# One mLSTM layer on one core: the per-head squares go from ScalarE to GpSimd, and a few steps at stage starts change places

## The reference

```
u = rmsnorm(x, mix_norm_g)
q, k, v, o_pre, gates = split(u @ w_in)          # 8 heads, 64 wide for q and k, 128 for v
per head, causal and stabilised:
    h = num / max(|den|, exp(-m))                # num 128 wide per head, den one number
h = merge_heads(_rms(h)) * norm_g                # _rms: divide by sqrt(mean(h^2) + 1e-6), per head
x = x + (h * sigmoid(o_pre)) @ w_out
x = x + (silu(n @ w_gate) * (n @ w_up)) @ w_down # n = rmsnorm(x, ffn_norm_g), 2816 wide inside
```

## Time and profile before

| what | value |
|---|---|
| median of the runs | 2179.42 us |
| the profiled execution | 2179.42 us, of which the span is 2177.8 us |
| PE busy | 2126.1 us, 98% of the span |
| PEld, DVE, ACT, POOL busy | 1766.0, 1431.5, 939.2, 252.5 us |
| chain that ended last | PE 89%, DVE 6%, ACT 2%, DMA 1% |
| granted TensorE clock, mean | 0.994 |

### The profile page before, as it was taken

One profiled execution on the slowest core, in us unless ns is written; L12 is line 12 of the kernel. 1 busy time (PEld: TensorE's weight loads), 2 busy tenths in 40 slices (PEclk: granted clock), 3 DMA queues, 4 the chain that ended last, 5 costly groups with the idle time before them and its releaser, 6 DMA issues.

```text
span 2177.8 us, 29479 instructions
## 1 busy us (share of the span) xinstructions
PE 2126.1 (98%) x10440; PEld 1766.0 (81%) x10440; DVE 1431.5 (66%) x2274; ACT 939.2 (43%) x1686; POOL 252.5 (12%) x357
## 2 busy tenths in 40 slices
PE   5999999999999999999999999899999999999999
PEld 4888878888888888788878888788888888888887
DVE  8775466686656565579687644767865756556764
ACT  4443664453333333345444346543533333333443
POOL 4111100020101010100122111001110101001000
PEclk8999999999999999999999999999999999999999
DMA  4333364213233324863524334532223332357443
GB/s 146 102 116 106 98 238 145 88 49 121 97 116 101 116 92 142 295 229 113 155 68 140 96 102 155 213 136 78 68 97 116 101 109 95 100 197 245 149 132 109
DMA packets 200289, 281.56 MB, mean 129 GB/s; under 512 B 12913, under 2 KB 131697, under 8 KB 200177
## 3 DMA queue, kind: packets, MB, share of 16 engines
q1 hardware_dynamic: 171696, 183.07, 26.6%
q0 software_dynamic: 28480, 97.02, 12.7%
HBM read 197.73 MB, written 82.31 MB: 129 GB/s over the span
## 4 chain that ended last, share of the span: by engine, by line
PE 89%; DVE 6%; ACT 2%; DMA 1%; issue 1%; SPq 0%; POOL 0%; DVEq 0%; POOLq 0%; ACTq 0%
PE ps L2179 13%; PE ps L2181 13%; PE ps L2182 13%; PE ps L1920 7%; PE ps L1924 7%; PE ps L1922 7%; PE ps L2227 6%; PE ps L2231 6%; PE ps L2229 6%; PE ps L1833 2%; PE ps L1835 2%; PE ps L1834 2%; PE ps L1840 1%; DMA g_in<-ops_hbm 1%; PE ps L2098 1%
## 5 line engine op out<-in xcount | busy, mean ns | idle before, releaser
L1671 DVE TENSOR_TENSOR ring<-raw_f,ring 128x512 fp32r<-128x512 f32 x308 | 211.4, 687 | 187.6 <-ACT ring L1107 186.5
L1107 ACT CAST ring<-raw_f 128x512 fp32r<-128x512 f32 x308 | 191.1, 622 | 208.0 <-PE ps L2182 194.0
L2179 PE MATMUL ps<-u_lo,ring 128*128 128x512 f32 x704 | 275.6, 391 | 2.2 <-DVE u_lo L1268 2.2
L2182 PE MATMUL ps<-u_hi,ring 128*128 128x512 f32 x704 | 274.1, 389 | 0.0
L2181 PE MATMUL ps<-u_hi,ring 128*128 128x512 f32 x704 | 273.9, 389 | 0.0
L2227 PE MATMUL ps<-ring,ring 128*128 128x512 f32 x616 | 240.9, 391 | 7.1 <-DVE ring L1750 7.1
L2229 PE MATMUL ps<-ring,ring 128*128 128x512 f32 x616 | 239.8, 389 | 0.0
L2231 PE MATMUL ps<-ring,ring 128*128 128x512 f32 x616 | 239.7, 389 | 0.0
L2179 PE MATMUL ps<-t_op,ring 128*128 128x512 f32 x528 | 205.9, 390 | 0.0
L2182 PE MATMUL ps<-t_op,ring 128*128 128x512 f32 x528 | 205.5, 389 | 0.0
L2181 PE MATMUL ps<-t_op,ring 128*128 128x512 f32 x528 | 205.4, 389 | 0.0
(11 more groups left out here) (219 smaller groups left out, 4198.8 us busy)
## 6 DMA issues: line engine op xcount, KB each, us to landing
ops_hbm<-kept POOLq DMA_DIRECT2D x154, 256.0 KB, 2.4
g_in<-ops_hbm SPq DMA_DIRECT2D x154, 256.0 KB, 2.7
raw<-in_ml_w_in_dram SPq DMA_DIRECT2D x24, 1024.0 KB, 5.3
proj_hbm<-pkept POOLq DMA_DIRECT2D x96, 256.0 KB, 2.7
raw_f<-in_ffn_w_gate_dram SPq DMA_DIRECT2D x44, 512.0 KB, 4.7
raw_f<-in_ffn_w_up_dram SPq DMA_DIRECT2D x44, 512.0 KB, 4.5
b<-in_ffn_w_down_dram SPq DMA_DIRECT2D x88, 256.0 KB, 4.9
x_in<-in_x_dram SPq DMA_DIRECT2D x16, 512.0 KB, 6.1
```

The lines of the kernel that those rows point to most:

```text
L1107: nc.scalar.copy(four(ring[slot][:, 0, :]), feed_source(q, s)).then_inc(w_hi_done, 1)
L1671: nc.vector.tensor_tensor(four(ring[slot][:, 1, :]), feed_source(q, s), four(ring[slot][:, 0, :].bitcast(F32)), ALU.subtract).then_inc(w_l ...
L2179: pe.matmul(banks(bank), wh, moved(kind, 1, k), start=(fresh and k == 0), stop=False, skip_group_check=True)
L2182: last = pe.matmul(banks(bank), wl, moved(kind, 0, k), start=False, stop=(k == 3), skip_group_check=True)
```

## The change

It has these parts:

- `squares(c)` is taken from ScalarE's list and put in GpSimd's, as a `tensor_tensor` multiplication of `num` by itself. It waits for the same counts. In chunk 0 it stands ahead of the `memset` of `v1[1]`, and `load_res(c)` is issued behind it.
- `SUMS_AT`: the second and third pair of sums are made one drain step earlier.
- At the start of a half ScalarE does `op_hi` 10 ahead of `proj_hi` 5, and VectorE `op_lo` 10 and both `proj_sums` ahead of `proj_lo` 5. In the second half VectorE also does `add_unit(1, 1)` ahead of `op_lo` 7, and `op_lo` 8 ahead of `proj_lo` 4.
- On TensorE `gates(0)` is done in one piece in the second half, ahead of turns 8 and 9 (before, it stood in two pieces of 8 between and behind them), and in the first half turn 9 stands ahead of the first half of projection 4.
- `keep_unit` of projection unit 6 goes one place later, behind `proj_hi` 11.

```diff
-SUMS_AT = {52: 0, 72: 1, 74: 2, 75: 3}
+SUMS_AT = {52: 0, 71: 1, 73: 2, 75: 3}
...
+                def squares(c):
+                    pool.wait_ge(num_kept, h * 16 + c * 2 + 2)
+                    if c:
+                        pool.wait_ge(h_turned, h * 8 + c)
+                    nc.gpsimd.tensor_tensor(hrow[:, :, :], num[:, :, 0:DV], num[:, :, 0:DV], ALU.mult)\
+                        .then_inc(sq_done, 1)
+                    if c == 0:
+                        pool.wait_ge(p_stored[1], h * 384 + 384)
+                        nc.gpsimd.memset(v1[1][:, :, DV:VW], 1.0).then_inc(ones_set, 1)
+                        pool.wait_ge(p_fed, h * PU + PU)
+                    if c < 4:
+                        load_res(c)
...
                 for c in range(TILES):
                     if c >= 3:
                         store_h(c - 3)
-                    if c < 4:
-                        pool.wait_ge(num_kept, h * 16 + c * 2 + 2)
-                        load_res(c)
+                    squares(c)
...
-                def squares(c):
-                    act.wait_ge(num_kept, h * 16 + c * 2 + 2)
-                    if c:
-                        act.wait_ge(h_turned, h * 8 + c)
-                    nc.scalar.activation(hrow[:, :, :], num[:, :, 0:DV], ACT.Square).then_inc(sq_done, 1)
...
-                    squares(c)
                     if c + 1 < TILES:
                         keep_v(c + 1)
...
+                op_hi(st, 10)
                 act.wait_ge(xn_done, st * TILES + TILES)
                 proj_hi(h, 5)
-                op_hi(st, 10)
...
-                if h == 0:
-                    gates(0)
-                    turn_unit(st, 7)
-                    turn_unit(st, 8)
-                else:
-                    turn_unit(st, 8)
-                    gates(0, 0, 8)
-                    turn_unit(st, 9)
-                    gates(0, 8, 16)
+                gates(0)
+                if h == 0:
+                    turn_unit(st, 7)
+                turn_unit(st, 8)
+                turn_unit(st, 9)
                 pe.wait_ge(op_lo_done, st * OP_UNITS + 9)
                 project(4, 0, 2)
-                if h == 0:
-                    turn_unit(st, 9)
                 turn_unit(st, 10)
```

More of the change, by code:

```diff
@@ L741, in load_res @@
                         .then_inc(res_loaded[q], 16)
-                pool.wait_ge(p_stored[1], h * 384 + 384)
-                nc.gpsimd.memset(v1[1][:, :, DV:VW], 1.0).then_inc(ones_set, 1)
-                pool.wait_ge(p_fed, h * PU + PU)
+                def squares(c):
[10 more added lines that the diff above has]
+                        load_res(c)
                 def store_h(i):
@@ L1007, in _ @@
                             split_out(0, k)
-                    if n == 5:
-                        keep_unit(*unit_of(6))
-                    if n > 6:
+                    if n >= 6:
                         keep_unit(g, q)
@@ L1462, in _ @@
                     proj_sums(h, 0, 0)
+                    add_unit(1, 1)
                     op_lo(st, 7)
-                    add_unit(1, 1)
+                    op_lo(st, 8)
                     proj_lo(h, 4)
-                    op_lo(st, 8)
                     dve.wait_ge(t_made_pool, st * 8 + 8)
+                    op_lo(st, 9)
                     proj_sums(h, 1, 0)
-                    op_lo(st, 9)
+                op_lo(st, 10)
                 proj_sums(h, 0, 1)
+                proj_sums(h, 1, 1)
                 proj_lo(h, 5)
-                proj_sums(h, 1, 1)
-                op_lo(st, 10)
                 op_lo(st, 11)
@@ L1927, in project, with gates @@
                         last.then_inc(p_fed, 1)
-                def gates(t, first=0, last_=24):
+                def gates(t):
                     pe.wait_ge(if_lo_done, h + 1)
@@ L1936, in gates @@
                             steps += [(k, u_lo[:, 0, k, :]), (k, u_hi[:, 0, k, :])]
[L1937 to L1941, removed]
+                    for i, (k, m) in enumerate(steps):
+                        last = pe.matmul(banks(gate_bank(t)), if_w[:, k, :], m, start=(i == 0), stop=(i == len(steps) - 1))
+                    last.then_inc(if_done, 1)
                 if h == 0:
```

## The result

Four runs of each kernel, in turn: 2196.1 us (2193.99 to 2196.44) after, 2180.94 (2179.38 to 2182.5) before. The ratio is 1.0064, interval 1.0052 to 1.0078: 11.3 to 17 us slower, 14 in the middle (the medians are 15.2 apart). The profiled execution of after took 2195.8 us, span 2194.1.

The account below looks back on a forecast made before the run. The prediction took TensorE, busy in 98% of the span, to bound the kernel. Squares 8.6, second half's start 4.4 and first half's 0.2 sum to 13.2 us on 2179.42: 2192.6 us, range 2185 to 2200 (8 in 10).

Parts of the forecast that it names:

- The square: In the chunks: the square on GpSimd takes 2.4 us and makes TensorE wait longer, 8.6 us for both halves.
- 4d − 2.5: TensorE's delay per half, summed over chunks 0, 1, 2 and 7: 4.3 us.
- d: Delay per chunk of VectorE's sum from moving the square to GpSimd: taken as 1.7 us, ends 0.4 and 2.7.
- The lock: In the chunks: GpSimd's square and VectorE's two-SBUF-input operations shut each other out; without this the wait is 0.2 us shorter.
- The second half's start: Gate products ahead of turns 8 and 9 give TensorE waits of 2.4 and 2.2 us; `gates(1)` 4.4 us later.
- `keep_unit` 6 at 0: Keeping projection unit 6 later costs 0 us, as TensorE does not wait in that stage.
- `SUMS_AT` at 0: Last steps: moved sums move VectorE's hold-ups by GpSimd, but as many remain; cost 0, bounds −1.1 to +1.1 us.
- The first half's +0.2: First half's start: turn 9 goes into the 5.31 us wait ahead of projection 4; `gates(1)` comes 0.2 us later.
- Rival 1: TensorE's clock falls in the longer waits of chunks 2 and 3, 7.2 us more: 2199.8 us; chance 0.13.
- Rivals 2 and 3: Square cheap, d = 0.4: 2185.6 us, chance 0.13; square meeting more traffic, d = 2.7: 2200.6 us, chance 0.05.
- rival 5: Second half's split start does nothing, so 4.4 us falls away: 2188.2 us; chance 0.07.
- Rival 4: Chunk 0: freed ScalarE does copy and decay matrix 1.06 us earlier, so not slower: 2179.8 us; chance 0.05.

Follow-up runs that it names:

- the eleven: Against the kernel before: 11 matmuls of no use in each half, inside TensorE's 4.3 us wait for the scaled rows; ratio 0.9987, 2178.28 us.
- the two edits: Against before: ScalarE's scale step of chunk 0 ahead of its decay matrix, first half's turn 9 in TensorE's wait ahead of projection 4; 0.998, 2176.59 us.

## Why the prediction was right, and where it was not

- **The place of the loss** was right: TensorE's waits for `kw` and the weights in chunks 2 and 3, nothing in the later ones, and two new waits at the second half's start.
- **The square** was mis-sized: 8.6 us forecast, 5.2 (3.3 to 7.2) measured. Twice the half-size operation, less 0.2, was too high a price: 2.4 against 1.89 us. The 2.25 us that the prediction estimates from the figure of the Trainium skill (page "GPSIMD Engine Reference", section "3.1 Elementwise — side-by-side cycle accounting") were too high as well; the measurement decides. Either the fixed part of the operation is not as small as the prediction has it, or reading one tile twice is cheaper than reading two: no run tells these apart. The formula 4d − 2.5 then fails at d = 1.03, because two of its four terms go below their covers (1.27 and 1.23) and are nothing; 2d per half is left, 4.1 in all, and that is what the waits of chunks 2 and 3 grew by. What is above it is the clock.
- **The lock** of VectorE by GpSimd was right to 0.03 us. The Trainium skill, page "SBUF — State Buffer", section "Who interferes with whom", says that the two hold each other off for a whole instruction; the trace agrees (1.77 us for an operation of 0.17).
- **The second half's start**: 4.4 forecast, 6.1 by landmarks (5.2 by the ratio, 3.3 to 7.2, with the first half's start in it). The waits were right within 0.3 us; missing was the clock behind the first, 1.7 us. The step "the gate products were the cover" is shown by the run with the gates alone.
- **`keep_unit` 6 at 0** failed: 2.4 us. The reason given, "TensorE does not wait in that stage", holds for before and says nothing of how near a wait it is. The row of ScalarE's next instruction (1.37 us of idling for VectorE, above) would have shown what the copy was moved behind.
- **`SUMS_AT` at 0**: right in the number, not in the reason. TensorE's waits in the last steps fell from 4.1 to 3.1 us, and the low clock behind the one of 2.92 us gave the gain back.
- **The first half's +0.2**: right. Turn 9 alone gave 1.2 us there; in the new lists `proj_lo` 5, behind `op_lo` 10 and the sums, takes it back in a wait of 1.9 us.
- **Rival 1**, the clock, had part of the truth: it fell behind both waits for the weights in the profiled execution of after. But it put the fall into chunks 2 and 3, and only the weights' wait had it, and not each time.
- **Rivals 2 and 3** are out with d = 1.03, and rival 5 with the 6.1 us. **Rival 4** is out too: the copy of `v` starts 1.33 us after `num` is complete in both kernels, and after, ScalarE idles 1.32 us ahead of it for the DMA.
- **The total** came out close by luck. The square's excess (3.4) nearly cancelled with the missing `keep_unit` (2.4) and what the starts cost above the forecast. The profiled execution of after is deceptive here: its chunks 0 to 3 lost 8.3 us by landmarks, which looks like the 8.6 forecast, but 4.2 of it are waits and most of the rest is the clock.

## What to carry to other kernels

Where the bounding engine has no wait, measure the slack before calling an edit free: compare when the last operand was ready with when it was used (76.33 and 77.83 for `keep_unit` 6, which moved by 3 us; 319.16 and 319.21 for the decay matrix, where 0.05 us is nothing). An instruction moved past another one takes over that one's wait, so look at the idle time ahead of the instruction that it is moved behind. And to fill a wait of TensorE can pay even with matmuls of no use (−2.8 us with the eleven), since behind an empty wait the clock may be at its low level. Last, when a total agrees with a forecast, measure its terms one by one.

## What the runs showed of the hardware

- GpSimd's multiplication of a 128x1024 tile by itself took 1.89 us beside VectorE's small operations.
- The length of a wait alone does not tell what TensorE's clock does behind it. The same wait had both outcomes in the two halves of one execution: 1.81 us (the eleven matmuls), 1.84 (the squares alone) and 2.96 (the two edits). It also held behind 2.43 and 2.59 us and fell behind 2.13, 2.20 and 2.36. Behind the wait of 4.3 us for the rows it fell in every half of every run that has this wait, and behind those of 1.67 to 1.74 us for the ring it held each time.
- The waits for the ring at about 919 and 1990 us carry much of the scatter of this kernel. With the same order there, the first was 2.43 us (before), 3.74 (with the eleven matmuls), 0.46 (two edits), and was not there with the squares alone and with turn 9 alone; the second was 0.64 us before and 3.77 with the eleven matmuls. With the squares alone, the 3.41 us lost by chunk 3 had come down to 0.93 at 1098 us. So landmarks have to be read stage by stage, and a difference of the ends of two profiled executions is uncertain by about 3 us (an estimate from these waits).
